# Sixteen experts' products: from split hi and lo weights to native fp32 on the array's two column halves

## The reference

```python
aff = sigmoid(t @ w_router)                      # 256 x 16
# best of 4 groups of 4 experts, then the top 2 in that group; gates sum to 1
for e in range(16):
    h = silu(t @ w1[e]) * (t @ w3[e])            # 1024 -> 512
    y = y + gates[:, e:e + 1] * (h @ w2[e])      # 512 -> 1024
h = layer_norm(ALPHA * h + y)
```

## Time and profile before

| | us |
|---|---|
| median of 3 runs | 1693.7 (1691.97 to 1694.32) |
| the profiled execution's own time | 1698.06 |
| its span in the trace | 1696.3 |
| TensorE (PE) busy | 1614.2, 95% |
| VectorE (DVE) busy | 1377.3, 81% |
| ScalarE (ACT) busy | 1034.4, 61% |
| chain that ended last, PE's share | 73% |
| HBM read | 418.26 MB |

### The profile page before, as it was taken

The page is one execution under the profiler, slowest core; times in us unless marked ns, Lnnn a source line. Parts: engine busy times, 40 slices in busy tenths (PEclk is TensorE's granted clock), DMA queues, the critical chain, the costliest instruction groups (busy, mean ns, idle before and its releaser), DMA issues.

```text
span 1696.3 us, 23297 instructions
## 1 busy us (share of the span) xinstructions
PE 1614.2 (95%) x9114; PEld 1370.4 (81%) x9114; DVE 1377.3 (81%) x2009; ACT 1034.4 (61%) x1530; POOL 122.2 (7%) x103
## 2 busy tenths in 40 slices
PE   7999999997999999999969989999999999999998
PEld 7878778876897878878757977899898788789987
DVE  4977999999788799999998977798777876675554
ACT  6356888887334488888864565544445556454443
POOL 0001111111000011111121000000002000000000
PEclk9997999999999999999989999999999999999999
DMA  8956999984555779998746633499883542235540
GB/s 343 346 192 254 378 398 363 384 358 184 196 214 208 297 306 369 389 371 349 304 154 225 227 122 139 147 354 347 321 319 113 185 149 100 100 149 181 191 174 26
DMA packets 58790, 420.91 MB, mean 248 GB/s; under 512 B 6625, under 2 KB 6689, under 8 KB 8370
## 3 DMA queue, kind: packets, MB, share of 16 engines
q1 hardware_dynamic: 58034, 417.19, 64.1%
q0 software_dynamic: 640, 2.14, 0.4%
HBM read 418.26 MB, written 1.05 MB: 247 GB/s over the span
## 4 chain that ended last, share of the span: by engine, by line
PE 73%; DVE 16%; ACT 9%; issue 2%; DMA 0%; SPq 0%; ACTq 0%; DVEq 0%
PE ps L794 71%; DVE lo L1918 7%; ACT hi L1478 3%; ACT AR L1819 2%; DVE AR L1911 2%; DVE AR L1908 1%; PE ps L880 1%; DVE ACC L1911 1%; PE ps L1366 1%; DVE X L1911 1%; PE ps L1340 1%; ACT AF L1666 0%; ACT AR L1831 0%; DVE AF L1911 0%; ACT AR L1642 0%
## 5 line engine op out<-in xcount | busy, mean ns | idle before, releaser
L1918 DVE TENSOR_TENSOR lo<-raw,hi 128x1024 fp32r<-128x1024 f32 x484 | 591.6, 1244 | 135.8 <-ACT hi L1478 134.2
L1478 ACT ACTIVATE hi<-raw 128x1024 fp32r<-128x1024 f32 x484 | 498.8, 1056 | 221.6 <-PE ps L794 216.3
L794 PE MATMUL ps<-hi,T 128*128 128x512 f32 x1364 | 490.5, 409 | 5.4 <-DVE T L1911 3.0
L794 PE MATMUL ps<-lo,T 128*128 128x512 f32 x916 | 361.8, 395 | 0.0
L794 PE MATMUL ps<-T,hi 128*128 128x256 f32 x1792 | 331.4, 286 | 10.8 <-DVE lo L1918 8.6
L794 PEld LDWEIGHTS ps<-hi,T 128*128 128x128 f32 x1364 | 260.0, 191 | 66.5 <-issue 12.4
L794 PEld LDWEIGHTS ps<-T,hi 128*128 128x128 f32 x1792 | 282.7, 193 | 22.3 <-DVE lo L1918 10.2
L794 PE MATMUL ps<-hi,AF 128*128 128x512 f32 x752 | 263.5, 399 | 0.4 <-DVE AF L2642 0.4
L794 PE MATMUL ps<-T,lo 128*128 128x256 f32 x896 | 254.1, 284 | 0.0
L794 PEld LDWEIGHTS ps<-lo,T 128*128 128x128 f32 x916 | 174.4, 190 | 40.0 <-issue 7.2
L794 PE MATMUL ps<-lo,AF 128*128 128x512 f32 x496 | 196.1, 395 | 0.0
(11 more groups left out here) (235 smaller groups left out, 1866.8 us busy)
## 6 DMA issues: line engine op xcount, KB each, us to landing
raw<-in_moe SPq DMA_DIRECT2D x98, 1024.0 KB, 7.9
AR<-in_moe SPq DMA_DIRECT2D x78, 1024.0 KB, 8.0
raw<-in_b_ff SPq DMA_DIRECT2D x64, 1024.0 KB, 4.9
raw<-in_ada SPq DMA_DIRECT2D x48, 1024.0 KB, 5.7
raw<-in_b_in SPq DMA_DIRECT2D x24, 1024.0 KB, 5.0
ACC<-in_moe SPq DMA_DIRECT2D x16, 1024.0 KB, 7.8
raw<-in_b_gate SPq DMA_DIRECT2D x16, 1024.0 KB, 4.8
raw<-in_ml_qk SPq DMA_DIRECT2D x8, 1024.0 KB, 5.8
```

The costliest lines, as they stand in the source:

```text
L794: return e.matmul(o, l, r, start=a, stop=z, skip_group_check=True)
L1478: e.activation(hi[n % NC][:, :], raw[place[c]][:, 1024 * half:1024 * half + 1024], ACT.Copy).then_inc(*to("hi", "hi", n))
L1918: tt(lo[n % NC][:, :], r, hi[n % NC][:, :], SUB).then_inc(*to("lo", "lo", n))
```

## The change

- All units of an MoE are `whole`: none is split, ACT's hi copies and DVE's lo subtractions of the 192 units of each stage go (177 of the 192 had them).
- The experts are taken two at a time, in pairs p = 0 to 7. XG holds native fp32 tokens, 64 columns per expert (the hi and lo gather products are now added up in one PSUM accumulation). Two products, one for each expert, go to output rows 0 to 63 and 64 to 127 of one bank, that is to the two halves of the array's columns, each with its own moving operand: `two_products`.
- The chunks of two experts are interleaved in DRAM (`_two`), chunk by chunk.
- `fold`, RS, the hi/lo split of the hidden state, POOL's TW and PTC go. The hidden state GR (64 rows each of two experts) is transposed by 4 products with the identity (`turn`) and copied by ACT to G2 in fp32. tanh, the two remaining DVE steps, y_hi, y_lo and scatter work on pairs (128 rows).
- The 40 KiB of the hi and lo rings are lent as five more places, 7 to 11, to chunks 11 to 80 of each stage, once the last unit before the stage has been used (`ring_free`). The first five splits of the next stage wait until they are given back. ACC and AR's stretch at 2048 come at chunks 16 and 17 (before: 8 and 11).
- The number of chunks, and everything outside the MoE stages, is unchanged.

The diff, cut to its core:

```diff
+        ring = [nc.alloc_sbuf_tensor_at(f"ring{i}", [128, 2048], F32, offset=nc.sbuf_base - 4 * 2048 * (NC - i)) for i in range(NC)]
...
+        raw += [x[:, :] for x in ring]
...
+        def ring_free(i):
+            return "used", unit_of[moe_at[i] - 1, 1][0]
...
-            XG = T2[:, :].rearrange("p (e k s) -> p e k s", e=4, k=8)
+            XG = TF[:, :].rearrange("p (g k e s) -> p g k e s", g=2, k=8, e=4)
...
-                def product(o, x, h, l, c, first, end):
-                    if l is None:
-                        return mm(o, x.bitcast(F32), h[:, c], first, end)
-                    mm(o, x, h[:, c], first, False)
-                    return mm(o, x, l[:, c], False, end)
+                def two_products(o, xs, ws, first, end):
+                    for s in range(2):
+                        ins = mm(o[64 * s:64 * s + 64, :], xs[s], ws[s], first, end)
+                    return ins
...
+                        x, n, half, us = a
+                        got = [unit(u)[0] for u in us]
+                        for j in range(4):
+                            k = 4 * half + j
+                            w.wait_ge(*after("gathered", i, x // 2, k // 2))
+                            ins = two_products(p, [m.XG[:, x // 2 % 2, k, 2 * (x % 2) + s, :] for s in range(2)],
+                                               [got[2 * s + j // 2][:, HALF[j % 2]] for s in range(2)], k == 0, k == 7)
...
+    for p in range(9):
+        for s in range(6):
+            if (p == 8 and s < 4) or (p == 0 and s > 3):
                 continue
+            us = []
+            for _ in range(4):
+                u, split = feed.unit()
+                us.append(u)
+                yield from split
+            if s < 4:
+                yield ("up", p, s // 2, s % 2, tuple(us))
             else:
+                yield ("down", p - 1, s - 4, tuple(us))
+            if s in (1, 3):
+                yield (("silu", "gated")[s // 2], p)
+            elif s > 3:
+                yield ("y", p - 1, s - 4)
+            yield from beside(p, s)
...
+                if n in given_back:
+                    for q in range(7, 7 + NC):
+                        for done in emptied(lent(given_back[n], q)):
+                            w.wait_ge(*after(*done))
...
+                    elif q > 6:
+                        w.wait_ge(*after(*ring_free(i)))
...
-    return {94: 0}.get(c, (0, 0, 0, 0, 1, 0)[c % 6]) if name.startswith("moe") else 0
+    return 3 if name.startswith("moe") else 0
...
-                        ((3, 3, 3), (1, 4, 95), (2, 5, 95), (4, 6, 95), (5, 7, 76), (0, 8, 95), (6, 11, 95))]
+                        ((3, 3, 3), (1, 4, 95), (2, 5, 95), (4, 6, 95), (5, 7, 76), (7, 11, 80), (8, 12, 80), (9, 13, 80),
+                         (10, 14, 80), (11, 15, 80), (0, 16, 95), (6, 17, 95))]
```

More of the change, by code:

```diff
@@ L292, in walk_moe @@
     yield ("x_lo", 1)
-    yield from feed.some_late(NC)
-    for k in range(4):
+    for k in range(3):
         yield ("gather", 0, k)
[L296 to L360, removed]
-                continue
[L362 to L373, removed]
-            else:
[L375 to L383, removed]
@@ L384, in walk_moe, with beside @@
-    while due:
-        yield from later(list(due))
+    def beside(p, s):
+        if s == 0:
+            if p == 0:
+                yield ("gather", 0, 3)
+                yield ("gates",)
+            if p in (0, 2, 4):
+                yield ("one_hot", p // 2 + 1)
+            if p == 1:
+                yield ("turn", 0)
+        if p > 1 and s == (0 if p < 8 else 4):
+            yield ("scatter", p - 2, 0)
+        if p > 1 and s == (1 if p < 8 else 5):
+            yield ("scatter", p - 2, 1)
+        if p == 0 and s == 1:
+            yield ("carry_lo",)
+        if p < 8 and s == 2:
+            yield ("maps", p)
+            yield ("gains", p)
+        if 0 < p < 8 and s == 4:
+            yield ("turn", p)
+        if p < 6:
+            for k, at in enumerate(((2, 3) if p == 0 else (3, 4)) if p % 2 == 0 else (0, 2)):
+                if s == at:
+                    yield ("gather", p // 2 + 1, 2 * (p % 2) + k)
@@ L697, in lent @@
             return max(c for c in uses[NR + p] if c <= until)
+        moe_at = [small["spare"][i][0][1] - 3 for i in range(2)]
+        given_back = {}
+        for c0, i in stops.items():
+            first = min(n for n, u in enumerate(plan.splits) if plan.units[u][0] >= c0)
+            given_back.update({n: i for n in range(first, first + NC)})
+        def ring_free(i):
+            return "used", unit_of[moe_at[i] - 1, 1][0]
         HALF = (slice(0, 512), slice(512, 1024))
@@ L1071, in moe @@
                         w.wait_ge(*after("gates", i))
[L1072 to L1075, removed]
+                        for q in range(2):
+                            c = 16 * q + 2 * x
+                            ins = mm(p[:, 0:4], places_of(x, q), m.ghl[:, c:c + 2, :].rearrange("p n h -> p (n h)"), q == 0, q == 1)
                         ins.then_inc(*to("tile", "gains", i, x))
@@ L1078, in moe @@
                     elif what == "up":
-                        x, n, uu, u = a
-                        if uu == 0:
+                        x, n, half, us = a
+                        if half == 0:
                             take("up", i, x, n)
                         p = PS[bank["up", i, x, n]]
[L1083 to L1087, removed]
@@ new lines, in moe @@
+                        if x:
+                            w.wait_ge(*after("gated_h", i, x - 1))
+                        e.activation(m.TT, PS[bank["up", i, x, 0]][:, :], ACT.Tanh, scale=0.5).then_inc(*to("func", "tanh", i, x))
+                    elif what == "turn":
+                        x = a[0]
+                        w.wait_ge(*after("turn", i, x))
+                        if x > 1:
+                            w.wait_ge(*after("down", i, x - 2, 1))
+                        e.activation(m.G2[x % 2].rearrange("p f e s -> p (f e s)"), PS[bank["turn", i, x]][:, :],
+                                     ACT.Copy).then_inc(*to("tile_out", "turned", i, x))
+                    elif what == "y":
@@ L2258, in moe @@
                         tt(m.ghl[:, :, 1], m.gate, m.ghl[:, :, 0], SUB).then_inc(*to("step", "gates", i))
-                    elif what == "gains_out":
+                    elif what == "gains":
                         x = a[0]
                         w.wait_ge(*after("gains", i, x))
-                        e.tensor_reduce(m.GS[:, x:x + 2], PS[bank["gains", i, x]][:, 0:4].rearrange("p (d h) -> p d h", h=2),
-                                        AX.X, ADD).then_inc(*to("step", "gain", i, x))
-                    elif what == "gate":
+                        for s in range(2):
+                            rows = slice(64 * s, 64 * s + 64)
+                            ins = e.tensor_reduce(m.GS[rows, x:x + 1], PS[bank["gains", i, x]][rows, 2 * s:2 * s + 2], AX.X, ADD)
+                        ins.then_inc(*to("step", "gain", i, x))
+                    elif what == "silu":
+                        x = a[0]
+                        w.wait_ge(*after("tanh", i, x))
+                        stt(m.TT, m.TT, 1.0, PS[bank["up", i, x, 0]][:, :], ADD, MUL).then_inc(*to("swiglu", "silu", i, x))
+                    elif what == "gated":
@@ L2281, in moe @@
+                        if x:
+                            w.wait_ge(*after("turn", i, x - 1))
+                        stt(m.GR, m.TT, 0.5, PS[bank["up", i, x, 1]][:, :], MUL, MUL).then_inc(*to("swiglu", "gated_h", i, x))
+                    elif what == "y":
                         x, n = a
-                        rows = slice(64 * (x % 2), 64 * (x % 2) + 64)
                         w.wait_ge(*after("y_hi", i, x, n))
-                        w.wait_ge(*after("gain", i, x - x % 2))
-                        stt(m.YL[rows, HALF[n]], PS[bank["down", i, x, n]][rows, :], m.GS[rows, x:x + 1], m.YH[rows, HALF[n]],
+                        w.wait_ge(*after("gain", i, x))
+                        stt(m.YL[:, HALF[n]], PS[bank["down", i, x, n]][:, :], m.GS[:, x:x + 1], m.YH[:, HALF[n]],
@@ L2295, in moe @@
                         for n in range(2):
[L2296 removed]
+                            w.wait_ge(*after("scatter", i, 7, n))
                             for t in range(2):
```

249 lines of the change are left out of this document (92 added, 157 removed).

## The result

The changed kernel takes 1582.15 us by the median of 4 runs (1575.34 to 1585.22), against 1693.45 before (1691.97 to 1694.32). The ratio is 0.934, with a 95% interval of 0.931 to 0.937: 111 us, 6.6% faster. The forecast was 1582. Its profiled execution was the fastest of the four, 1575.34 us with a span of 1573.4.

What follows compares the result with a forecast made beforehand. PE bound the kernel's MoE stages, DVE and DMA close behind; after the change PE and DMA bounds would meet. 1698.1 - 115 for both stages + 3 behind them = 1586, less 4.4 for the median: 1582 us, range 1568 to 1640.

Steps and rivals of the forecast that it cites:

- its first case: MoE stages: column halves run together and the DMA keeps its full-queue rate; 1582 us, 1568 to 1605, chance 0.66.
- TensorE's k-step: MoE stages: two native products on the array's column halves run together, 0.86 us for two experts, before 0.94.
- C: MoE k-steps: the halves overlap only in part at 512 columns, 1.0 us a step; kernel 1635, chance 0.06.
- D: MoE k-steps: the halves don't overlap, 1.72 us a step; kernel 1908, chance 0.05.
- TensorE's sum: One MoE stage, first gather to last scatter: steps 165.1 us plus gathers, scatters, turns, mode changes and others, total 213.
- DMA: MoE weight loads: 2.5 us a chunk with the queue full, making the DMA the bound in the steady part.
- rival B: MoE stages: the DMA doesn't hold its rate, 380 GB/s, 2.76 us a chunk; kernel 1618 by the median, chance 0.15.
- The prefilled places: Ahead of each MoE stage: 18 chunks find a place beforehand instead of 13, each chunk taking 2.5 us.
- rival E: Lent places idle or PE stalled: 13 instead of 18 chunks ahead, DMA 12.5 us later per stage, 1610; chance 0.08.
- The meeting of the bounds: End of each MoE stage: PE and DMA bounds meet within 3 us, so 3 us added; ends 358 and 802.5.
- Behind the stages: Norm after each MoE stage: five hi copies on ACT wait for late weights, 1.5 us each, 3 in all.
- Base: Whole kernel: starts from the profiled execution's 1698.1 us; the median of the runs is 4.4 lower.

Runs made afterwards that it cites:

- Experiment 5: The kernel before with all MoE units whole in native fp32, one expert at a time on the whole array, without column halves: 1966.08 us, ratio 1.162.
- experiment 1: The changed kernel run again without any edit, for a second profile: 1581.57 us median of 5 runs, ratio 0.9339.
- experiment 8: The changed kernel with work between the steps gathered into fewer places, 28 breaks a stage instead of 35: 1580.67 us median, ratio 0.9336.

## Why the prediction was right

The forecast was 1582 with 1568 to 1640 around it, and the mechanism was the one of its first case. Step by step:

- *TensorE's k-step.* 0.86 us for two experts, taken from the attention's 256-column products. The trace shows 0.43 us between pairs of 512 columns. Rivals C and D are out. Experiment 5 shows that the gain hangs on it, as the forecast said: 408 us a stage without the halves, where 410 followed from the same prices.
- *TensorE's sum.* It is given as 213 us a stage, but its terms add up to 214.2. Of these, 1.3 are for the half clock, which this profile didn't have at the first gathers of the first stage: 212.9 against 215.4 measured. The missing 2.5 are in small terms. The first interval of a step behind a break is 0.48 instead of 0.43 (146.84 to 147.32), besides the change of mode: 35 times 0.05, 1.8. Groups of gathers and of maps start slower too, with a first interval of 0.22 instead of 0.12 for a gather (145.70 to 145.92), some 1.6 more together. Against that, the 1.1 for the first eviction cost nothing, since the steps follow the first gathers after 0.2 us.
- *DMA.* 2.5 us a chunk from windows of 10 and 30 us. The slices of the plateaus have 420 to 422 GB/s, 2.49 us, for as long as the queue is full, so rival B is out. (By the forecast's own terms B's second stage would end at 823, not 819, and that of a chunk of 2.93 us at 839, not 832; both totals would be some 4 us higher, and the range would not change.) The figure of 358 GB/s for a core, which the forecast quoted from the Trainium skill, "DMA: Bandwidth & Descriptors", section "Where 436 GB/s comes from", isn't seen on this core over some 190 us of full queue.
- *The prefilled places.* Five places at 2.5 us a stage: 12.5 predicted for their absence (rival E, 1610), 12 measured, 1604.
- *The meeting of the bounds.* 358 and 802.5 were the ends, from starts at 141.7 and 586.9: 216 us each, with 3 added for the meeting. Measured 215.4 and 217.8. TensorE's waits for landings were 0 and 0.8 us in this profile, 1.6 and 0.6 in the second, so the 3 for the meeting were too much; they made good the 2.4 by which the 213 was short of 215.4. The second stage's 217.8 also has 1.5 for the half clock at its first gathers. That the total came out within 1 us is partly this luck.
- *Behind the stages.* 3 us were taken for hi copies that wait for late weights. They didn't wait: the norm and the turn behind the first stage take 9.35 us, 9.25 before (414.86 to 424.11), and ACT stood idle for 1.86 us ahead of the norm's rows. In the timeline the row answers to the earlier trace rows:

```profile
352.68 3.90 ACT L1444 ACTIVATE hi<-raw 128x1024 fp32r<-128x1024 f32 x4 [0.27 <-issue]
...
358.43 1.45 ACT L1476 ACTIVATE AR<-ps,TINY 128x512 f32<-128x512 f32 x2 [1.86 <-DVE TINY L1867]
```

  ACT's four copies are done at 356.6, 1.9 us before the norm wants ACT. The forecast had five copies ahead of the norm's rows; the fifth stands behind them here, at 366.06, and its chunk had landed at 356.5, 1.7 us later than forecast (both counted from the stage's start) and still before the norm's rows. The term should have been 0.
- *Base.* The forecast took 4.4 us off the profiled time for the median. The profiled execution of before was at the slow end (1698.06 against 1687.6 to 1698.4 in the later runs), that of after at the fast end. Only the medians compare.

## What to carry to other kernels

Two products with 64 stationary columns each, on the two halves of TensorE's columns, cost what one costs (0.86 us for native fp32 of 512 columns), if they stand within four instructions of each other in the queue; that halves native fp32 and makes it cheaper than a split into two fp32r products, but native fp32 alone on the whole array was 16% slower than the split. When an engine stops being the bound, ask at once what the freed memory buys: here the rings of the removed split were worth 22 of 111 us as places for weights, because the DMA bound stood just behind TensorE's. And when two bounds meet, as they do now, an edit to one of them moves nothing that can be measured.

## What the runs showed that was not expected

- TensorE fills the free column half from up to four matmul instructions ahead in its queue, not only from the next one: blocks of four cost nothing that can be measured, blocks of eight cost 5.26 instead of 3.49 us a step.
- A wait for a landing can stand in the views as "issue". In the kernels here such pauses in the middle of a step (1.44 us in experiment 1, 1.43 in experiment 8) ended 0.1 us after a chunk's landing, and only the landing's time told so.
- The time of the part behind the second stage, whose code is the same in all of them, ranged from 829.7 to 836.0 us over the ten profiles, with 53 to 67 us of it at the half clock, at places that shift from launch to launch. A single profile's difference of less than some 6 us therefore proves nothing in this kernel, and the changed kernel's runs scattered over 13 us (1574 to 1587, with experiment 8) around medians that agreed within 2.
